# An eighth slot and a fifth high buffer for the expert weights of a two-network kernel

## What is computed

```python
def moe_ffn(x, router_w, w1, w3, w2):        # 8 experts, 1024 -> 3584 -> 1024
    logits = (xt @ router_w).astype(F32)
    top_v, top_i = lax.top_k(logits, TOP_K)  # TOP_K = 2
    top_w = jax.nn.softmax(top_v, axis=-1)
    gates = jnp.sum(jax.nn.one_hot(top_i, N_EXPERTS, dtype=F32) * top_w[..., None], axis=1)
    y = jnp.zeros_like(xt)
    for e in range(N_EXPERTS):
        y = y + gates[:, e:e + 1].astype(x.dtype) * swiglu(xt, w1[e], w3[e], w2[e])
```

## Time and profile before

| | us |
|---|---|
| median of three runs | 2359.77 |
| lowest, highest | 2358.21, 2362.82 |
| profiled execution | 2354.97 |
| its span | 2353.1 |
| expert rounds 0 to 7, in that execution | 435.7 to 1441.7 |
| first network before them | 435.7 |
| second network behind them | 911.4 |
| DMA, mean over the span | 247 GB/s |

### The profile page before, as it was taken

One profiled execution on the slowest core, in us unless ns is written; L12 is line 12 of the kernel. 1 busy time (PEld: TensorE's weight loads), 2 busy tenths in 40 slices (PEclk: granted clock), 3 DMA queues, 4 the chain that ended last, 5 costly groups with the idle time before them and its releaser, 6 DMA issues.

```text
span 2353.1 us, 29291 instructions
## 1 busy us (share of the span) xinstructions
PE 2300.6 (98%) x11179; PEld 1890.8 (80%) x11179; DVE 1812.7 (77%) x2343; ACT 1391.2 (59%) x1588; POOL 31.7 (1%) x44
## 2 busy tenths in 40 slices
PE   9999999999999999999999998999999999999998
PEld 7788887888778887788778776888888888888887
DVE  5964567898975558998999898899765669987655
ACT  4444534677865447877887785565544545654543
POOL 0000000000000000000000000000000000000000
PEclk9999998999999999999999999999999999999999
DMA  8366542799986569999999995654566565455653
GB/s 283 106 224 188 182 156 101 277 364 356 411 290 215 197 232 367 407 401 374 396 408 381 369 404 221 198 157 144 172 202 185 183 210 162 122 175 168 201 187 124
DMA packets 198220, 582.10 MB, mean 247 GB/s; under 512 B 17227, under 2 KB 26583, under 8 KB 183608
## 3 DMA queue, kind: packets, MB, share of 16 engines
q1 hardware_dynamic: 195772, 571.87, 69.2%
q0 software_dynamic: 1872, 6.82, 0.8%
q10 hardware_dynamic: 428, 1.45, 0.2%
HBM read 579.02 MB, written 1.07 MB: 247 GB/s over the span
## 4 chain that ended last, share of the span: by engine, by line
PE 81%; DVE 9%; DMA 4%; ACT 4%; issue 1%; ACTq 0%; POOL 0%; POOLq 0%; SPq 0%; DVEq 0%
PE tile L903 21%; PE tile L905 21%; PE tile L904 21%; PE aux L1026 4%; DMA units<-in_moe_w 3%; DVE units_parts L2508 3%; PE aux L1370 2%; PE tile L1484 2%; PE tile L1485 2%; ACT high L1895 1%; DVE nat_parts L2508 1%; DVE k_buf_parts L2508 1%; DVE q_buf_parts L2508 1%; PE tile L1382 1%; PE tile L1384 1%
## 5 line engine op out<-in xcount | busy, mean ns | idle before, releaser
L2508 DVE TENSOR_TENSOR units_parts<-units,high 128x1024 fp32r<-128x1024 f32 (+3 forms) x357 | 523.8, 1485 | 102.9 <-ACT high L1895 100.1
L1895 ACT ACTIVATE high<-units 128x1024 fp32r<-128x1024 f32 (+3 forms) x357 | 447.6, 1272 | 177.8 <-PE tile L905 59.6
L904 PE MATMUL tile<-units_parts,acts 128*128 128x512 f32 (+2 forms) x1392 | 533.5, 383 | 0.0
L903 PE MATMUL tile<-high,acts 128*128 128x512 f32 (+2 forms) x1012 | 401.0, 396 | 6.3 <-DVE units_parts L2508 3.7
L905 PE MATMUL tile<-high,acts 128*128 128x512 f32 (+2 forms) x1012 | 389.8, 385 | 0.0
L904 PEld LDWEIGHTS tile<-units_parts,acts 128*128 128x128 f32 x1392 | 263.3, 189 | 48.0 <-issue 1.0
L903 PEld LDWEIGHTS tile<-high,acts 128*128 128x128 f32 x1012 | 191.5, 189 | 44.5 <-DVE units_parts L2508 5.7
L905 PEld LDWEIGHTS tile<-high,acts 128*128 128x128 f32 x1012 | 191.1, 189 | 38.5
L904 PE MATMUL tile<-units_parts,zbuf_parts 128*128 128x512 f32 x456 | 177.4, 389 | 0.0
L905 PE MATMUL tile<-high,zbuf_parts 128*128 128x512 f32 x368 | 143.3, 389 | 0.0
L2508 DVE TENSOR_TENSOR units_parts<-units,gbuf_parts 128x2048 fp32r<-128x2048 f32 x48 | 109.9, 2289 | 16.6 <-ACT gbuf_parts L1895 16.5
(11 more groups left out here) (527 smaller groups left out, 4868.5 us busy)
## 6 DMA issues: line engine op xcount, KB each, us to landing
units<-in_moe_w SPq DMA_DIRECT2D x192, 1024.0 KB, 7.2
units<-in_w_in SPq DMA_DIRECT2D x134, 512.0 KB, 3.8
units<-in_w_ff SPq DMA_DIRECT2D x128, 512.0 KB, 3.7
q_buf<-in_moe_w SPq DMA_DIRECT2D x48, 1024.0 KB, 7.2
k_buf<-in_moe_w SPq DMA_DIRECT2D x48, 1024.0 KB, 7.8
nat<-in_moe_w SPq DMA_DIRECT2D x48, 1024.0 KB, 6.9
units<-in_ffn_w SPq DMA_DIRECT2D x48, 512.0 KB, 4.3
units<-in_w_out SPq DMA_DIRECT2D x32, 512.0 KB, 3.5
```

Source lines behind the costliest of these rows:

```text
L903: nc.tensor.matmul(bank, lhs[0], high, start=start, stop=False)
L904: nc.tensor.matmul(bank, lhs[0], low, start=False, stop=False)
L1895: nc.scalar.activation(high_slot(SG[0], n) if wide_ else high_slot(SG[0], n)[:, 0:cols], halves(weights) if wide_ else weights[:, 0:cols], ...
L2508: V.tensor_tensor(low, weights, high, ALU.subtract).then_inc(SG[0].low_ready, 1)
```

## The change

Before, seven raw slots and four high buffers hold expert units. After, there are eight and five, so that the lead is four.

- The eighth raw slot is rows 0 and 1 of `gain`. It is lent in two stretches, written as spans of units for the class `Ring`: units 0 to 83, free once one unit is done, and units 136 to 272, free once 129 are done. Outside them the seven own slots rotate. `Ring` gives each unit the slot that was used longest ago. With these spans the slot's last unit is 272, and `GAIN_FREE` is 273.
- The fifth high buffer is `bias2`. Its content is stored to HBM (`bias_kept`) in front of the last output weights of the first network, and loaded again behind the first six units of the second.
- `EXPERT_LEAD` becomes 4. SP loads four units of the next round ahead of the routing's register reads in place of three.
- POOL's gain loads wait for `GAIN_FREE`, 273 units, where they waited for 168.

```diff
-EXPERT_COLS, EXPERT_UNITS, EXPERT_HIGHS = 2048, 7, 4
+EXPERT_COLS, EXPERT_UNITS, EXPERT_HIGHS = 2048, 8, 5
+EXPERT_OWN = 7
...
-assert MOE_UNITS % EXPERT_UNITS == 0
+assert MOE_UNITS % EXPERT_OWN == 0
+GAIN_LENT = [(0, LARGE * MOE_UNITS, 1),
+             ((LARGE + 1) * MOE_UNITS + TURN_AFTER + 2 + EXPERT_OWN, (N_EXP - 2) * MOE_UNITS + MOE_UNITS // 2,
+              (LARGE + 1) * MOE_UNITS + TURN_AFTER + 2)]
+EXPERTS = Ring(ROUNDS * MOE_UNITS, EXPERT_OWN * [[(0, ROUNDS * MOE_UNITS, 0)]] + [GAIN_LENT])
+GAIN_FREE = 1 + EXPERTS.last[EXPERT_OWN]
...
-        bias2 = sb("bias2", [P, NSA_H, SEQ])
+        bias2, bias2_parts = shared("bias2", [P, NSA_H, SEQ])
...
+        expert_ring.append(gain[:, 0:2, :].rearrange("p i n -> p (i n)"))
+        expert_lows.append(gain_parts[:, 0:2, :].rearrange("p i n -> p (i n)"))
+        expert_highs.append(halves(bias2_parts[:, :, :].rearrange("p h t -> p (h t)")))
...
+        bias_kept = nc.dram_tensor("bias_kept", (P, NSA_H, SEQ), F32)
...
-                k = m % EXPERT_UNITS
-                return expert_ring[k], expert_lows[k], expert_loaded[k], m // EXPERT_UNITS + 1
+                k = EXPERTS.slot[m]
+                return expert_ring[k], expert_lows[k], expert_loaded[k], EXPERTS.loads[m]
...
-                shared_ = lent[m - 3] if 3 <= m < EXPERT_UNITS else 0
-                return max(n - EXPERT_UNITS + 1, shared_)
+                if m < EXPERT_OWN:
+                    return lent[m - 3] if m >= 3 else 0
+                return len(STREAM1) + EXPERTS.free[m]
...
-                shared_ = lent[m - 1] if 1 <= m < EXPERT_HIGHS - 1 else 0
+                shared_ = lent[m - 1] if 1 <= m <= len(lent) else 0
...
+                    sp.wait_ge(S.unit_done, FF1_AT)
+                    sp.dma_start(bias_kept.ap(), bias2[:, :, :]).then_inc(bias2_stored, 16)
                     wide(S, A["w_out"][l], 0, D - P)
...
                         load_params2(l)
+                        if l == 0:
+                            sp.dma_start(bias2[:, :, :], bias_kept.ap()).then_inc(bias2_loaded, 16)
...
                     wait(act, SG[0].unit_done, done_for_high(SG[0], n))
+                    if expert_unit(SG[0], n) == EXPERT_HIGHS - 1:
+                        act.wait_ge(bias2_stored, 16)
...
-                    pool.wait_ge(S.unit_done, len(STREAM1) + (LARGE + 2) * MOE_UNITS)
+                    pool.wait_ge(S.unit_done, len(STREAM1) + GAIN_FREE)
...
                 bank = aux_in()
+                dve.wait_ge(bias2_loaded, 16)
```

## The result

| | before | after |
|---|---|---|
| median, us | 2358.99 | 2375.89 |
| lowest | 2356.34 | 2368.27 |
| highest (one more run of before took 9668.07) | 2362.82 | 2380.15 |
| profiled execution, and its span | 2354.97, 2353.1 | 2374.07, 2372.2 |
| mean granted clock of the timed runs | 0.9946 | 0.9885 |

The change makes the kernel 0.66% slower: the ratio is 1.0066, interval 1.0050 to 1.0081. The ratio is not the quotient of the medians, which is 1.0072; that of the means, without the run of 9668.07 us, is 1.0067. I had forecast 2358.1, in a range from 2348 to 2365. The clock of before is the mean over the 27 runs that stood beside the first experiments, that of after over its six.

A forecast was written before the change was run, and what follows sets the result against it. Matmuls filled 98% of the span, with the DMA as full as TensorE in the short rounds. Terms summed to -1.65 us: 2353.3 profiled, 2358.1 for the median, in a range from 2348 to 2365.

The forecast's parts named there:

- Four ahead, at the exits: Ends of rounds 1, 3, 5: `back_low` waits behind one more landing, nearly cancelling the slot's gain; 0.35 us lost net.
- -0.5, +0.15 and 0: Net terms at the exits from rounds 1 to 2, 3 to 4, 5 to 6: 0.5 us won, 0.15 lost, 0.
- rival B: Short rounds' landings don't move, DMA being saturated; exit waits paid in full, 7.2 us lost, 2365.7 us; chance 0.14.
- Long DVE work: Round 4: one more unit in hand covers TensorE's 0.79 us wait behind `find_extra`; 0.8 us won.
- The start: DVE splits one unit more before `lows_gathered`, so TensorE's first expert product comes later; 1.3 us lost.
- Round 7: Last short round, none behind it: shorter waits at its head and slots free earlier; 1.8 us won.
- Gain loads: Three 512 KB loads move from the head of round 4 to round 6, where the DMA has gaps; 0.
- bias2: Its store behind the first network's last input load and its reload in the second network cost 0.
- The eighth slot: Entering rounds 1, 3 and 5, landings come 2.56, 2.4 and 2.56 us earlier, a gain spent at the exits.
- rival A: The exits don't bind because DVE has run ahead, so slots keep their 7.5 us gain; 2351.0 us; chance 0.25.

The follow-up runs named there:

- e7: The changed kernel, four ahead in all rounds, but only three splits in front of `back_out` and `back_low` ending rounds 1, 3 and 5: 2368.82 us.
- e4: The changed kernel with a lead of three in short rounds 1, 3, 5 and 7 and at their exits, four in the others: 2354.61 us.
- e1: The changed kernel with all of the change except the lead, which stays at three: 2350.37 us, ratio 0.9958 to the kernel before.
- e6: e1 with the fourth split in front of `back_out` and `back_low` at the ends of rounds 1, 3 and 5 alone: 2357.41 us.
- e14: e1 with TensorE alone waiting, before each fold of the short rounds, until the second unit from there is split too: 2419.78 us.
- e12: e7 with four small filler products on TensorE before each fold of the short rounds: 2362.12 us.
- e10: The changed kernel, with the fourth split in the short rounds moved behind the hidden tiles' copies, `back_out` and `back_low`: 2353.20 us.
- e11: The kernel before with only the fifth high buffer and its bias2 transfers added, seven slots, three ahead: 2353.59 us, ratio 0.9985.
- e5: The changed kernel with filler products on TensorE, 12 before the scatter or `other_rows` of rounds 2, 4, 6, six before each short-round fold: 2377.97 us.

## Why the prediction was wrong, step by step

**The step that failed: "Four ahead, at the exits".** It took three exits for all the places where the fourth split delays something that TensorE waits for, and every wait at its length. Inside the rounds the fourth split had no price at all.

- It says that queued behind the fourth unit are "`back_low`, the scatter and the rest of the round". The copies of the hidden tiles stand behind `used(...)` in just the same way, in front of every fold of the short rounds, and the fold waits for them. This was left out; it is 14.2 of the 25.5 us that a lead of four costs (e7 against e4). The long rounds add 4.2 (e4 against e1). Together these are 18.4 us with no term in the sum. The sum is off by 16.9 + 1.65 = 18.5; that the two agree so closely is luck, since the other terms miss by some us each and cancel. The rule that I had written down myself, what is written behind such a call waits for the load of its last unit, I applied at one place of its kind.
- The price of the exits themselves came out near. The -0.5, +0.15 and 0 are what is left of 7.5 us won by earlier landings and 7.15 lost by `back_low` behind one landing more. The second is 7.0 and 7.1 us by e6 and e7. The first is less: with a lead of three, rounds 1, 3 and 5 are together 5.1 us shorter (the fifth buffer has its share in that), and the third unit of the lead begins at 668.13 - 562.9 = 105.2 us of round 1 and 986.72 - 878.0 = 108.7 of round 3, against 106.8 and 110.3 before, which is 1.6 earlier in both and not 2.56 and 2.4. With a lead of four it began at 672.40 - 565.2 = 107.2, 0.4 later than before, and at 996.34 - 887.8 = 108.5, 1.8 earlier. The fourth came 2.72 and 3.31 us after it, not 2.56. So the landings moved, which rival B denies, but by less than the forecast needed.
- The -0.5 is also misread. It puts the 5.62 us of the other exit behind the landing at 666.11, but the trace has 6.13 there, for DVE was behind: it split without a pause and came to that unit 2.47 us after ScalarE's start, not 1.95. With its own length the term is 0.

```profile
666.38 2.28 DVE L2508 TENSOR_TENSOR k_buf_parts<-k_buf,high 128x2048 fp32r<-128x2048 f32 x1
668.58 2.28 DVE L2508 TENSOR_TENSOR nat_parts<-nat,high 128x2048 fp32r<-128x2048 f32 x1
670.78 1.40 DVE L3115 SCALAR_TENSOR_TENSOR gbuf_parts<-tile,small,gbuf_parts 128x512 fp32r<-128x512 f32 x2
```

- No term had the clock in it. The 27 runs of the kernel before show what it is worth: eight at 0.996 or 0.997 average 2356.0 us, nine at 0.992 or 0.993 average 2361.8, which is 1.6 us for 0.001. The changed kernel runs at 0.0061 less: an estimate of 10 of its 17 us. For e7 against e4, 0.0079 less gives 12.6 of 14.2. That longer waits before the folds bring the clock down is shown by e14, and that work in them brings it back by e12; how much of the 17 us is the clock and how much the waits is not settled closer than this estimate, since each filler costs time of its own.

The Trainium skill has the rule in TensorE: Matmul & The Clock Gate, Part 1: the gated clock is the resting state, and it is activity that lifts it. The trace agrees, with 0.33 us for a load behind two waits of 1.18 and 2.13 us and 0.19 in front of them. The page also puts the penalty of warming up under 1% of a typical span; 10 of 2359 us is 0.4%, under that, and larger than every term of my sum. For e14 the same estimate, 0.0198 less than e1, gives 32 us or 1.3%, over it.

**The other terms.** *Long DVE work*: the wait of 0.79 at `find_extra` is gone, as forecast. But the extra split stands before `gate_hidden` too: 2.1 us at L1043 where there had been 0.4, in round 6. The long rounds lose 4.2 us (e4 against e1) where I had them gain 0.8. *The start*: TensorE's first expert product waits for `lows_gathered`,

```profile
441.89 0.50 PE L920 MATMUL tile<-gbuf_parts,acts 128*128 128x512 f32 x1 [0.90 <-DVE acts L3062]
```

0.90 us of the 1.3 forecast. It is 6.2 us later than before in all. The clock in the first network was 0.79 in 360 to 400 us against 0.83, which is at most 1.6 us; the rest is not explained. This product begins at 433.74 us in e10's profiled execution, behind the same wait of 0.90, and at 440.19 in that of e1, which has no such wait but a clock of 0.71 and 0.61 in the 20 us before. So the place moves by more than the term from one execution to another, and no run shows the 1.3. *Round 7* was to be 1.8 shorter; it is 1.7 longer, and 0.4 shorter with a lead of three. *Gain loads* went out at 1290.72 us in round 6 without a wait beside them, and *bias2* cost less than the buffer brought (e11), both in line with the forecast.

**The eighth slot.** I had its gain spent at the exits. With a lead of three it is not spent: the three shorter short rounds stay won, and the fifth buffer gives some more (e11 against before; where, no row here shows). e1 came to 2350.4, where rival A, "the slots keep their gain", stood at 2351.0. That they are so near is luck in part: A had 7.5 us for the slot in rounds 1, 3 and 5 where 5.1 came, 1.8 for round 7 where 0.4 came, nothing for the fifth buffer, and its reason, that DVE has run ahead, was for a lead of four. What holds of A is that the slot's gain is kept if nothing else moves; it was the lead, which came with the fifth buffer, that took all of it and 17 us more.

## What to carry to other kernels

A deeper buffer and a longer lead are two changes. On an engine with one fixed order, "one more unit ahead" puts one more wait for a transfer in front of everything else that the engine does: list all of it, at every call, before you price one place. Keep the copies that another engine waits for in front of the last split ahead (e10), or leave the lead alone and take the buffer (e1, 0.42% faster than the kernel before). And where the DMA sets the pace, look at how TensorE's idle time is cut. Here many waits of 0.5 us left its clock whole, and so nearly did three single ones of 2.5 us (e6); a dozen of 1 to 3 us before the folds did not (e7, e14).

## What the runs showed that I had not expected

- The lead has a sharp optimum: in the short rounds two ahead costs 37 us against three, and four 21.
- The eighth slot is worth 27.6 us at a lead of four and 3.2 at three (25.9 and 6.4 by the ratios). A resource can look valuable because it mends what another part of the same change broke.
- From a lead of three to one of four the waits of TensorE in round 1 fell from 12.1 to 9.1 us, and the round grew from 105.0 to 106.2. The sum of waits said less than the granted clock beside it, 1.00 and 0.97.
- A plain 32-bit matmul over 256 columns is two instructions in the trace, 0.46 us together (e5's row), twice what I had sized it by.
